# Last expert combined by products instead of through DRAM, and a second attention layer without the queries of its meta rows

## What is computed

```
for layer in range(DEPTH):                 # DEPTH = 2
    h = hybrid_layer(h, pos, ...)          # h: 16 + 256 rows
return rms_norm(h, final_g)[:, N_META:]
```

```
gates = sum(one_hot(top_i) * softmax(top_v))       # 256 x 8, two entries a row
for e in range(8):
    out = out + gates[:, e:e+1] * swiglu(t, wg[e], wu[e], wd[e])
```

## Time and profile before

| | us |
|---|---|
| median of 3 runs | 1765.38 |
| profiled execution, its own time | 1765.0 |
| span of its trace | 1763.2 |
| first attention layer, 0 to 188 | 188 |
| second attention layer, 188 to 376 | 188 |
| first mixer and norms, 376 to 490 | 114 |
| dense SwiGLU, 490 to 676 | 186 |
| second mixer and routing, 676 to 781 | 105 |
| eight experts, 781 to 1736 | 955 |
| after the last expert's products | 27 |

### The profile page before, as it was taken

The page is one execution under the profiler, slowest core; times in us unless marked ns, Lnnn a source line. Parts: engine busy times, 40 slices in busy tenths (PEclk is TensorE's granted clock), DMA queues, the critical chain, the costliest instruction groups (busy, mean ns, idle before and its releaser), DMA issues.

```text
span 1763.2 us, 27386 instructions
## 1 busy us (share of the span) xinstructions
PE 1686.0 (96%) x10014; PEld 1480.7 (84%) x10014; DVE 1408.5 (80%) x1607; ACT 1152.2 (65%) x1297; POOL 253.0 (14%) x261
## 2 busy tenths in 40 slices
PE   8999899989899999899999999999999999999993
PEld 7888898889799999788888888888888888888883
DVE  7666666759866667868898898988998988989885
ACT  5563555456654446677777777777777777777773
POOL 2212022128310003600010010000100100101000
PEclk9999999999899999999999999999999999999997
DMA  7322442245455464359999999999999999999993
GB/s 302 120 85 85 160 139 97 72 155 182 162 173 191 131 214 152 126 195 378 379 368 373 379 387 365 372 391 385 360 391 387 375 374 372 385 378 367 393 386 132
DMA packets 71329, 476.86 MB, mean 270 GB/s; under 512 B 8405, under 2 KB 9077, under 8 KB 19413
## 3 DMA queue, kind: packets, MB, share of 16 engines
q1 hardware_dynamic: 67781, 463.25, 70.0%
q0 software_dynamic: 3184, 11.55, 1.8%
q10 hardware_dynamic: 288, 1.05, 0.1%
HBM read 469.53 MB, written 6.29 MB: 270 GB/s over the span
## 4 chain that ended last, share of the span: by engine, by line
PE 75%; issue 9%; DVE 8%; ACT 3%; POOL 3%; DMA 1%; SPq 0%; DVEq 0%; POOLq 0%; ACTq 0%
PE bank L451 24%; PE bank L453 23%; PE bank L452 23%; DVE wlo L442 2%; ACT whi L437 2%; PE bank L1096 1%; POOL cacc L2234 1%; DVE msb L1747 1%; DVE bank L1777 1%; DVE sm L1667 0%; PE bank L730 0%; DMA ys<-y_slots 0%; POOL pr L2150 0%; PE bank L674 0%; PE bank L1068 0%
## 5 line engine op out<-in xcount | busy, mean ns | idle before, releaser
L442 DVE TENSOR_TENSOR wlo<-raw,whi 128x2048 fp32r<-128x2048 f32 (+2 forms) x453 | 1000.8, 2219 | 177.7 <-ACT whi L437 176.5
L437 ACT ACTIVATE whi<-raw 128x2048 fp32r<-128x2048 f32 (+2 forms) x453 | 838.0, 1850 | 219.0 <-PE bank L453 218.8
L451 PE MATMUL bank<-whi,hthi 128*128 128x512 f32 x896 | 354.1, 395 | 1.7 <-DVE htlo L2077 1.7
L453 PE MATMUL bank<-whi,htlo 128*128 128x512 f32 x896 | 350.1, 391 | 0.0
L452 PE MATMUL bank<-wlo,hthi 128*128 128x512 f32 x896 | 349.7, 390 | 0.0
L451 PE MATMUL bank<-uhi,whi 128*128 128x272 f32 (+2 forms) x1072 | 315.1, 294 | 4.0 <-DVE wlo L442 3.5
L453 PE MATMUL bank<-uhi,wlo 128*128 128x272 f32 (+2 forms) x1072 | 306.3, 286 | 0.0
L452 PE MATMUL bank<-ulo,whi 128*128 128x272 f32 (+2 forms) x1072 | 305.8, 285 | 0.0
L451 PEld LDWEIGHTS bank<-uhi,whi 128*128 128x128 f32 (+1 forms) x1072 | 201.9, 188 | 7.2 <-DVE wlo L442 4.8
L452 PEld LDWEIGHTS bank<-ulo,whi 128*128 128x128 f32 (+1 forms) x1072 | 202.3, 189 | 0.7
L453 PEld LDWEIGHTS bank<-uhi,wlo 128*128 128x128 f32 (+1 forms) x1072 | 202.1, 189 | 0.0
(11 more groups left out here) (354 smaller groups left out, 2128.6 us busy)
## 6 DMA issues: line engine op xcount, KB each, us to landing
raw<-in_wm SPq DMA_DIRECT2D x338, 1024.0 KB, 7.1
raw<-in_w SPq DMA_DIRECT2D x66, 1024.0 KB, 5.0
raw<-in_w SPq DMA_DIRECT2D x18, 768.0 KB, 4.3
raw<-in_w SPq DMA_DIRECT2D x16, 704.0 KB, 4.2
raw<-in_w SPq DMA_DIRECT2D x14, 512.0 KB, 3.6
ys<-y_slots SPq DMA_DIRECT2D x4, 512.0 KB, 5.3
raw<-in_w SPq DMA_DIRECT2D x2, 576.0 KB, 3.7
hT<-in_hT SPq DMA_DIRECT2D x2, 544.0 KB, 6.1
```

Of the source, the lines that this page charges most:

```text
L437: act.activation(whi[:, n % RING, 0:c], raw[:, n % RAW, 0:c], ACT.Copy).then_inc(hi_ready, 1)
L442: dve.tensor_tensor(wlo[:, n % RING, 0:c], raw[:, n % RAW, 0:c], whi[:, n % RING, 0:c].bitcast(F32), ALU.subtract).then_inc(lo_ready, 1)
L451: pe.matmul(out, s_hi, m_hi, start=start, stop=False, skip_group_check=shared)
L453: return pe.matmul(out, s_lo, m_hi, start=False, stop=stop, skip_group_check=shared)
```

## The change

Five parts:

1. **Last expert unrolled and left on the chip.** The loops run over 7 experts, and the last is written out behind them. It prepares no next expert: no gather, no splits and loads of two more units (`load_unit`, `split_hi`, `split_lo` for pos + 2 >= UM). Its choice matrix `pick` is turned (`turn_pick`) and kept as `pickT`. Its last down chunk goes column half by column half (`down_by_halves`), so that columns 0 to 511 are finished first. Then `place` multiplies `pickT` with `yt`, four fp32 products of 128 x 128 by 512 columns, columns 0 to 511 for both token groups ahead, and VectorE adds each to `xt`.
2. **Slots read early.** SP loads `ys` right behind the last weight unit; VectorE adds it to `xt` in `settle`, before it scales the last rows. As the last expert's slots are never written, GpSimd clears `y_slots` with four DMAs (`clear_slots`) during the dense SwiGLU, and VectorE waits for them at the second mixer.
3. **ScalarE scales half.** VectorE scales columns 0 to 511 of `yt`, ScalarE the rest, from bank 6.
4. **Final norm by halves.** ScalarE squares each half as it comes; GpSimd makes mean and epsilon of the first half (`first_ms`), which is the bias of the root over the second.
5. **Second layer without meta rows.** `leaving(1)` is columns 16 to 271: queries, gates, scores of the meta tile, values, head sums, mix, output and residual leave the 16 columns out; keys and values keep them.

The diff, cut to its core:

```diff
+        def leaving(l):
+            return slice(META, LEN) if l == LAYERS - 1 else slice(0, LEN)
@@ SP
-            with sp.Fori(0, EXPERTS) as it:
+            with sp.Fori(0, LAST) as it:
                 expert(it)
-            sp.wait_ge(scattered, EXPERTS + 1)
+            expert(LAST, 0)
+            sp.wait_ge(scattered, EXPERTS)
+            load_rows()
             sp.wait_ge(count_ready, 1)
@@ TensorE, project
+                take = leaving(l) if TILE_OF[i][0] in "qz" else slice(0, LEN)
                 for k in range(KD):
-                    mm = three_pass(pe, bank[i % 2][:, 0:LEN], hi[:, k, cols], lo[:, k, cols],
-                                    uhi[:, k, :], ulo[:, k, :], k == 0, k == KD - 1)
+                    mm = three_pass(pe, bank[i % 2][:, take], hi[:, k, cols], lo[:, k, cols],
+                                    uhi[:, k, take], ulo[:, k, take], k == 0, k == KD - 1)
@@ TensorE, turn_probs
-                pe.transpose(bank[6][0:META, 3 * P - META:3 * P], b[0:META, 0:META], ident[0:META, 0:META]).then_inc(t_done, 1)
+                if l < LAYERS - 1:
+                    mm = pe.transpose(bank[6][0:META, 3 * P - META:3 * P], b[0:META, 0:META], ident[0:META, 0:META])
+                mm.then_inc(t_done, 1)
@@ TensorE, experts
+                def down_by_halves(c):
+                    pe.wait_ge(atlo_ready, it * CHUNKS + (c + 1))
+                    views = [weights(EXPERT_UNITS.index(("down", c, part))) for part in range(2)]
+                    for half in range(2):
+                        cols = slice(half * 512, (half + 1) * 512)
+                        for part, (hi, lo) in enumerate(views):
+                            for i in range(2):
+                                f = 2 * part + i
+                                mm = three_pass(pe, bank[5 + half][:], athi[:, c % 2, f, :], atlo[:, c % 2, f, :], hi[:, i, cols], lo[:, i, cols],
+                                                False, f == 3)
+                        mm.then_inc(unit_done, 1)
+            def place():
+                pe.wait_ge(rows_ready, 5)
+                for half in range(2):
+                    pe.wait_ge(yt_ready, EXPERTS + half)
+                    for tt in range(2):
+                        pe.matmul(bank[2 * tt + half][:], pickT[:, tt * P:(tt + 1) * P], yt[:, half * 512:(half + 1) * 512],
+                                  start=True, stop=True).then_inc(placed, 1)
@@ ScalarE
+            expert(LAST, True)
+            act.activation(warm[:, 7:8], eps[:], ACT.Sqrt)
+            act.wait_ge(slot_ready, EXPERTS)
+            act.wait_ge(unit_done, EXPERTS * UM + UNIT_MOE)
+            act.wait_ge(yt_ready, EXPERTS)
+            act.activation(yt[:, 512:D], bank[6][:], ACT.Copy, scale=row_gate[:]).then_inc(yt_ready, 1)
             with act.If(fullest > P):
...
+            for half in range(2):
+                for tt in range(2):
+                    act.wait_ge(sum_ready, 2 * half + tt + 1)
+                    act.activation(outn[:, tt, half * 512:(half + 1) * 512], xt[:, tt, half * 512:(half + 1) * 512], ACT.Square,
+                                   accum_out=ssq[:, half, tt:tt + 1]).then_inc(ssq_ready, 1)
             for tt in range(2):
+                act.wait_ge(ssq_ready, 2 + tt + 1)
+                act.wait_ge(first_ms_ready, tt + 1)
+                act.activation(rms[:, tt:tt + 1], ssq[:, 1, tt:tt + 1], ACT.Sqrt, bias=first_ms[:, tt:tt + 1], scale=1.0 / D).then_inc(rms_ready, 1)
@@ VectorE, last expert
+                    if last and kind == "down" and c == CHUNKS - 1:
+                        settle(part)
...
+                    if last and kind == "down" and c == CHUNKS - 1:
+                        dve.wait_ge(slot_ready, it + 1)
+                        dve.wait_ge(unit_done, it * UM + (UNIT_MOE + pos))
+                        dve.tensor_scalar(yt[:, 0:512], bank[5][:], row_gate[:], None, ALU.mult).then_inc(yt_ready, 1)
...
+            def settle(tt, times=1):
+                step = 4 * (times - 1) + 2 * tt
+                dve.wait_ge(ys_landed, 16 * 2 * TOP_K * times)
+                dve.tensor_tensor(ys[:, tt, 0, :], ys[:, tt, 0, :], ys[:, tt, 1, :], ALU.add).then_inc(result_step, 1)
+                dve.wait_ge(result_step, step + 1)
+                dve.tensor_tensor(xt[:, tt, :], xt[:, tt, :], ys[:, tt, 0, :], ALU.add).then_inc(result_step, 1)
...
+            expert(LAST, True)
+            dve.wait_ge(result_step, 4)
+            for half in range(2):
+                for tt in range(2):
+                    dve.wait_ge(placed, 2 * half + tt + 1)
+                    own = xt[:, tt, half * 512:(half + 1) * 512]
+                    dve.tensor_tensor(own, own, bank[2 * tt + half][:], ALU.add).then_inc(sum_ready, 1)
+            dve.wait_ge(sum_ready, 4)
             with dve.If(fullest > P):
@@ GpSimd
+            def clear_slots(source):
+                for i in range(2 * TOP_K):
+                    pool.dma_start(slots_dram[i * P:(i + 1) * P, :], source[:]).then_inc(zeroed, 16)
...
+                if L == 0:
+                    pool.wait_ge(unit_done, UNIT_FF)
+                    pool.memset(zero[:], 0.0).then_inc(const2_ready, 1)
+                    pool.wait_ge(const2_ready, CONST2 + 1)
+                    clear_slots(zero)
```

More of the change, by code:

```diff
@@ L488, in out_tiles, with entering, query_tiles @@
             return range(d, d + U1_TILES[j])
+        def leaving(l):
+            return slice(META, LEN) if l == LAYERS - 1 else slice(0, LEN)
+        def entering(q):
+            return leaving(q - 1) if q else slice(0, LEN)
+        def query_tiles(l):
+            tiles = [(t,) + tile for t, tile in enumerate(QTILES)]
+            return tiles[1:] if l == LAYERS - 1 else tiles
         def by_token(L):
@@ L562, in _, with expert @@
                 load_unit(sp, UNIT_MOE + j, source=io["wm"][0, j])
-            def expert(it):
-                for j in range(2, UM + 2):
+            def expert(it, ahead=2):
+                for j in range(2, UM + ahead):
                     e = it % EXPERTS if j < UM else (it + 1) % EXPERTS
@@ L669, in diff_scores @@
                     pe.wait_ge(masked, l * MAPS + m0)
-                for q0, rows, c0, keys in reversed(QTILES):
+                for t, q0, rows, c0, keys in reversed(query_tiles(l)):
                     for h in range(2):
@@ L1069, in gather, with expert @@
                 mm.then_inc(gather_done, 1)
-            def expert(it):
+            def expert(it, last=False):
                 def weights(pos):
@@ L1121, in expert @@
                     if c == SELECT_C:
-                        select(it + 1)
-                    if c == CHUNKS - 1:
+                        if last:
+                            turn_pick()
+                        else:
+                            select(it + 1)
+                    if c == CHUNKS - 1 and not last:
                         gather(0, it + 1)
@@ L1126, in expert, with turn_pick @@
                         down(c - 1)
-                gather(1, it + 1)
-                down(CHUNKS - 1)
+                if last:
+                    down_by_halves(CHUNKS - 1)
+                else:
+                    gather(1, it + 1)
+                    down(CHUNKS - 1)
+            def turn_pick():
+                pe.wait_ge(pick_ready, EXPERTS)
+                for tt in range(2):
+                    mm = pe.transpose(bank[7][:, tt * P:(tt + 1) * P], pick[:, tt, :], ident[:])
+                mm.then_inc(rows_turned, 1)
+            def place():
[5 more added lines that the diff above has]
+                                  start=True, stop=True).then_inc(placed, 1)
             select(0)
-            with pe.Fori(0, EXPERTS) as it:
+            with pe.Fori(0, LAST) as it:
                 expert(it)
-            pe.wait_ge(htlo_ready, 2 * EXPERTS + 2)
+            expert(LAST, True)
+            place()
             pe.wait_ge(count_ready, 1)
@@ L1486, in expert @@
                         rows_hi(CHUNKS - 1)
-                    split_hi(act, UNIT_MOE + pos + 2, it, UM)
+                    if not last or pos + 2 < UM:
+                        split_hi(act, UNIT_MOE + pos + 2, it, UM)
                     if part == 0:
@@ L1503, in _ @@
             gathered_hi(1, 0)
-            with act.Fori(0, EXPERTS) as it:
+            with act.Fori(0, LAST) as it:
                 expert(it)
@@ L1685, in difference @@
                 m = 2 * p
-                for t, (q0, rows, c0, keys) in enumerate(QTILES):
+                for t, q0, rows, c0, keys in query_tiles(l):
                     cols = slice(c0, c0 + keys)
@@ L2285, in _ @@
             pool.wait_ge(nt_stored, 32)
-            with pool.Fori(0, EXPERTS) as it:
-                expert(it)
+            with pool.Fori(0, LAST) as it:
+                expert(it, 1, 16)
             pool.wait_ge(count_ready, 1)
@@ L2290, in _ @@
             with pool.If(fullest > P):
+                pool.wait_ge(sum_ready, 4)
```

(14 more changed lines are left out.)

217 lines of the change are left out of this document (135 added, 82 removed).

## The result

The changed kernel takes 1745.3 us, the median of 4 runs (1744.24 to 1746.61), the kernel before beside it 1765.58 us. The ratio is 0.9885 with a 95% interval of 0.9868 to 0.9903: 20.3 us faster. The prediction was 1744.4 us with a range of 1739.5 to 1751.0. The profiled execution is the slowest of the four: 1746.61 us. Its span is 1744.8 us.

What follows compares the result with a forecast made beforehand. TensorE, busy 1686 of 1763.2 us, was taken as the bound, idle at the end. 8.5 (layer) + 12.7 (end) - 0.2 = 21.0 off 1765.0 gives 1744.0; the median, 0.4 above, 1744.4 us; range 1739.5 to 1751.

Steps and rivals of the forecast that it cites:

- The layer: Second attention layer without meta rows: 9.2 us less TensorE work, of which 8.5 us was taken as gain, bounds 5 to 12.
- the term for the products of queries and gates: Second layer: 384 products stream 256 instead of 272 columns, each 0.0093 us shorter, part of 5.4 us with the output's.
- Rival 1: Second layer: the gain runs into its 11.75 us of waits and wins 2 instead of 8.5 us, 1751; chance 0.12.
- Rival 3: Second layer: waits shrink too and a half-clock stretch goes, 1741 us; chance 0.1.
- The smaller terms: Second layer: 12 transposes dropped 1.8 us, meta tile of the scores 1.5, 21 fp32 products losing 16 columns 0.5.
- The end: From the last expert's down products to the span's end: the end comes at 1750.5 instead of 1763.2, winning 12.7 us.
- just as late as TensorE, costs nothing: Last expert: VectorE's four slot additions end at 1736.5, half 0 scaled by 1737.3, beside TensorE's 1737.1; no cost.
- VectorE's branch decides, not the norm: Behind the last addition: VectorE's skipped branch takes 2.47 us, to 1744.5, later than ScalarE's root at 1743.1.
- Rival 2: Last down products: the new 2.2 us stall halves TensorE's clock, 1.8 us more, place up to 3.9 more; chance 0.25.
- At nothing: Clearing the slots in the dense SwiGLU costs nothing; value_load ahead of the last expert is put at 0.2 us.
- Rival 4: Last expert: new code stalls each of its 42 units by about 2.47 us, adding 70 us, 1814; chance 0.02.
- Rival 5: At the end: the loads of ys come late and settle holds back everything, so no change; chance 0.02.

Runs made afterwards that it cites:

- e3: Changed kernel with ScalarE's early table load for the root moved behind its branch and a one-column VectorE marker behind VectorE's branch; 1743.82 us.
- e4: Changed kernel with the last expert's last down chunk unit by unit instead of by column halves, yt waiting for both units; 1743.7 us.
- e2: Changed kernel with only the second layer's query and gate products streaming 272 columns again; 1744.76 us.
- e1: Changed kernel with the second layer's 16 meta queries put back, 272 columns everywhere, the new end kept; 1750.7 us.
- e8: Changed kernel with the slots cleared twice, VectorE waiting for both rounds; 1743.57 us.
- e5: Changed kernel run again without any edit; 1743.92 us.
- e12: Changed kernel with only the tile warm widened from 8 to 24 columns, later tiles 64 bytes further on, no instruction added; 1765.45 us.
- e6: Changed kernel with VectorE scaling both halves of yt, ScalarE taking its branch and loading the root's table while TensorE still multiplies; 1742.17 us.
- e7: e6 with the last down chunk unit by unit and GpSimd adding the first token group's slots; 1741.65 us.
- e9: Changed kernel with 16 short activations at ScalarE's start and warm widened to 24 columns, moving later tiles 64 bytes; 1764.16 us.
- e10: Changed kernel with 32 short activations at ScalarE's start and warm widened to 40 columns, moving later tiles 128 bytes; 1764.15 us.
- e11: Changed kernel with 64 short activations at ScalarE's start and warm widened to 72 columns, moving later tiles 256 bytes; 1744.46 us.

## Why the prediction was right, and where it was off

**The layer** (8.5, bounds 5 to 12). It is 8.1 in the two profiled executions, 8.5 with e3 and 9.7 with e4 in the changed kernel's place. TensorE's busy time in the layer fell from 174.99 to 166.57 us, by 8.4 where the sum has 9.2, and its idle time grew by 0.3, from 11.67 to 12.00. How the 9.2 are made up is less certain: the term for the products of queries and gates, 3.6 of the 5.4, was measured only as something between 1 and 3.4 (e2). The groups of TensorE's instructions by form in the layer, with what ended the idle time before them, before and after:

```profile
L451 PE MATMUL bank<-mixhi,whi 128*128 128x272 f32 x64 | 19.8, 309 | 4.7 <-DVE wlo L442 2.5 <-DVE mixlo L1709 2.1
```

```profile
L456 PE MATMUL bank<-mixhi,whi 128*128 128x256 f32 x64 | 20.3, 318 | 4.0 <-DVE mixlo L1814 2.0 <-DVE wlo L447 2.0
```

Rival 1, that the gain runs into waits, is refuted. Rival 3, that a half-clock stretch goes, came in one place and was undone in another: from 260 to 276 us the granted clock was 0.79 before and is 0.89 now, but from 360 to 380 it fell from 0.96 to 0.74, and over the layer it is 0.96 instead of 0.97. With 0.98 in both, e1 and e8, the layer gains 185.86 - 176.95 = 8.9. Where that second stretch is shorter (e4 with 0.83, e8 with 0.91 there, both with 0.89 in the first) the layer takes 176.9 us. The smaller terms (transposes, scores, fp32 products) were not measured one by one; e1 less e2 gives 185.86 - 181.27 = 4.6 for them and the output's products together, where the sum has 1.8 + 1.5 + 0.5 + 1.8 = 5.6, before the 0.7 that I took off; but e1 ran at 0.98 and e2 at 0.95, so this 4.6 is as much too small as e2's 3.4 may be too large.

**The end** (12.7). It won 11.9. The steps, one after the other:
- TensorE half a microsecond earlier, the stall of 2.2 for the second `wlo`, 24 products: measured 2.14, and down products done 1.3 later than before (forecast 1.2).
- `settle` "just as late as TensorE, costs nothing": VectorE has half 0 scaled at 1730.29, and TensorE is busy with half 1 until it begins `place` at 1730.55. The two are level to 0.3 us, and e4 shows it from the other side: with TensorE done 2 us earlier `place` began only 0.1 sooner behind the last `wlo`.
- From the last down product to the last addition the forecast had 1742.0 - 1737.1 = 4.9 and it took 1734.87 - 1730.7 = 4.2. `place` was 3.59 instead of 3.9: the 0.13 that the prediction adds to each product for the switch of weights stands in none of its rows, and a product takes some 0.86 (the last two additions start 0.86 apart), nearly the 0.85 in proportion alone. And `place` began 0.15 ahead of the last down product's end, not 0.2 behind it.
- **The step that failed** is "VectorE's branch decides, not the norm". The 2.47 us of SP's branch were put on VectorE, where 0.68 was measured (e3), and ScalarE's branch was left out, though it stands on the path too and further ahead. There it costs 1.81, and two table loads of 1.28 follow, of which the prediction had none: it took the early load of the root's table at its word. From the last addition to the reciprocal the forecast had 2.47, and it took 1738.85 - 1734.87 = 4.0. The first error was too much and the second too little, so 1.5 is left of both.
- From there to the end: 6.0 forecast, 5.95 measured. In sum 4.2 + 4.0 + 5.95 = 14.1 instead of 13.4.

The Trainium skill ("Runtime: NRT & Kernel Launch", Instruction fetch mechanics) says that a taken branch whose target isn't in the fetched pages has to wait for it. The runs agree as far as they go (an instruction transfer in every gap, the gap gone when the code moves), and add what the prediction missed: the same skip may wait or not. On ScalarE it took 1.8 to 2.05 us in the changed kernel, e2, e3, e4, e5, e8 and e12, and nothing in e1, e6, e7, e9, e10 and e11; on VectorE it took 0.68.

**Rival 2**, that the new stall halves TensorE's clock, had 0.25 and 1.8 us. The stall is in eleven profiles (all but e4 and e7), with 2.11 to 2.14 us each. In nine the clock stayed; in e10 and e12 it did not. This is e12:

```profile
1746.00:1748.00 2.00, 2.00 (x6) 1.51 (x5) 2.00 (x2) 0.00 (x0) 0.00 (x0) 0.53 0.00 0
1748.00:1750.00 2.00, 2.00 (x7) 1.63 (x6) 1.97 (x3) 0.00 (x0) 0.00 (x0) 0.62 0.00 0
```

The down products start every 0.43 us there instead of 0.23, eight of them, and the tail is 1.6 us longer (21.6). The mechanism is real and its price was right, 1.6 against 1.8. e4, whose TensorE stalls 2.15 us in front of `place` instead, has the lower clock behind it too, for 1.8 us. So it came in three of twelve profiles with such a stall.

**At nothing.** For `clear_slots` e8 confirms it. `value_load` (0.2 in the sum) leaves no gap in front of the last expert. Rival 4, new code for each unit, is refuted: from 1611 to 1730.7 us TensorE is busy 117.56 of 119.70, idle only in the stall. Rival 5 is refuted by the rows of `ys`: the loads took 7.9 to 10.2 us to land, more than the 7.08 that was forecast, and were still more than 5 us early.

**The number.** It was 1744.4, against 1745.3 and, run again later, 1743.92. The forecast had 0.4 too much for the layer and 0.8 too much for the end (12.7 against 11.9). That it came within 1 us is partly luck. At the end 0.7 too little gain up to the last addition stands against 1.5 too much behind it. And the prediction didn't think of where the tiles lie at all: with them 64 bytes further on (e12) the same change wins nothing. The changed kernel's operands of the experts lie where they lay before, since its new tiles stand behind them (`first_ms`) or in a scope that is closed ahead of them (`zero`), and the pace stayed; the prediction did not ask for it.

## What to carry to other kernels

A branch that is skipped is priced for each engine that takes it, and the question is where it stands in that engine's program: ahead of the last wait it is free; behind it, whatever it costs in that layout of the code is paid. A table loaded early must survive up to its use. In the changed kernel the root's table was loaded ahead of the branch, and another was loaded behind it for squares that run with the root's table in e3 and e6; that the skipped branch between is the reason is my reading, and no run tests it alone. Before a difference of one per cent is put down to an edit, look at the pace of the matmuls in a stretch that the edit didn't touch: a tile that grows by 64 bytes can move it.

## What the runs showed of the hardware that was not expected

- Tiles of the experts, the stationary operands among them, moved by 64 or 128 bytes: 512-column products start every 0.233 instead of 0.227 us, with the granted clock at 1.00 in both; moved by 256 bytes, 0.227. In this kernel that is 20 us, all that the change had won (e9, e10, e12 against e11). Streamed operands moved by 64 bytes: 256-column products start every 0.1178 instead of 0.1200 us (e9, e12).
- ScalarE's skipped branch: 1.8 to 2.05 us or none, by where its code lies (e12 against e9 to e11), with an 8 KB transfer on an instruction queue inside each gap.
- GpSimd's additions of 128 x 1024 (3.19 and 4.31 us) beside VectorE's split of 128 x 2048: 3.9 instead of 2.29 us (e7).
- A TensorE stall of 2.11 to 2.15 us is followed by the lower clock in three of twelve profiles (e4, e10, e12) and by the higher one in nine.
